# Feed-forward of a decoder layer: token sums in place, down-weight sums made in the up part, sample sums in other banks

## The chip, the cores and the metric

The kernel runs on one core of one Trainium2 chip. The metric is device time in microseconds (us). Before the change it is 1657.48 us, the median of three runs (1655.96 to 1666.1). The core has five engines that run side by side: TensorE (PE), VectorE (DVE), ScalarE (ACT), GpSimd (POOL) and SyncE (SP), which here only issues DMA transfers. Each engine takes its instructions in the order in which they are written; between engines, order is made by semaphores: one instruction adds to a count, another engine waits until the count is reached.

## The reference, cut to what matters

The program is one layer of a decoder: a mixer (retention and latent attention), then a gated feed-forward with a convolution, then a final norm. The change is in the feed-forward alone. It works on 1072 tokens: 16 meta and 1024 prompt tokens, and 32 sample tokens (8 samples of 4), with D = 1024 and F = 2816.

```python
def conv_ffn(h, buf, w_up, conv_w, conv_b, w_down):
    u = h @ w_up                                  # 1024 -> 2 * 2816
    up = jnp.concatenate([buf, u], axis=1)
    c = conv_b
    for j in range(3):                            # causal, one weight per column
        c = c + conv_w[j] * up[:, j:j + T]
    a, g = jnp.split(c, 2, axis=-1)
    y = (jax.nn.silu(g) * a) @ w_down             # 2816 -> 1024
    return y, up[:, up.shape[1] - 2:]
```

Around it stand the norm ahead of it, the residual, h + y, and the last RMSNorm, all in float32.

## The kernel before, in words

**Arithmetic.** A float32 product is made of three matmuls. Each operand is split into a high part (a copy rounded to the matmul type, made by ACT) and a low part (operand minus high part, made by DVE or POOL); hi x hi, hi x lo and lo x hi are added up. On top of that, both big products are cut into 2 x 2 blocks and done by seven block products in place of eight, in the order `PRODUCTS = ("m1", "m5", "m6", "m3", "m7", "m2", "m4")`, called p = 0 to 6. For that, sums and differences of the blocks of both operands are needed.

**Up part.** 22 steps (n = 0 to 21), each for 128 columns of the a half and 128 of the g half of `w_up`. Tokens are in two halves of 532. Steps 0 and 1 are done without the block trick (`plain_part`), steps 2 to 21 with it (`step`). The normed tokens lie in SBUF as `xh` and `xl`; their block sums, four blocks (0 to 3) of four slices of 128x532, are made once, into `th` (high) and `tl` (low): by DVE (`t_slice`, L2489 to L2509: blocks 0, 1 and 3 of slice k), POOL (`t3_slice`, L2191 to L2197: block 2) and ACT (`t_hi`, L2337 and L2340: the high parts), while TensorE works on the plain steps. `tmp`, where sums are worked out, has room for four slices and lies in the same memory (`scr`) as `raw_d`, the down weights for the samples, and beside `chain`. TensorE's p = 1 of step 2 waits for all 16 low parts.

One up step: SP loads the weights into `raw` (`load_up`, L2033, two transfers of 512 KB), once all splits of the step before are done, since there is one `raw`. POOL makes four sums of 128x512 (`sums`, L2149, L2151, L2154, L2155), the middle ones in place in `chain`, so that each waits for the split of the one before; ACT makes seven high parts (`hi_part`, L2271), DVE seven low parts (`lo_part`, L2475), TensorE seven products of 24 matmuls (`passes`, L2699 to L2702). ACT copies PSUM to `u` (`first_out`, L2285, `second_out`, L2299), DVE adds the other products to it (`add_second`, L2517, `add_first`, L2524); p = 5 of the next step waits for `add_second`, as it writes the bank that is read there. Then follow the convolution (`tap2` on ACT, `taps` on DVE), `silu` (ACT), `gate` (DVE), and SP stores the step's rows of the activation into DRAM (`store_act`, L2039, 512 KB). POOL also does small work (`keep`, `params`).

**Samples.** Their down product is not in block form. ACT copies the samples' columns of two steps into `few` (`few_part`, L2330). SP loads two blocks of 128 rows of `w_down` (`load_down`, L2047, 1 MB) into `raw_d`, and TensorE runs 4 narrow matmuls at four column positions into PSUM bank 6 (`strips`, L2776), after every second step. In the down part DVE copies the bank out (`quads`, L2661), TensorE adds the four strips up (`sum_few`, L2800) in banks 4 and 5 (`SUM_BANKS`), and DVE adds `hs`, the residual (L2667); the first matmul of p = 1 waits for that (`few_added`).

**Down part.** 77 steps, `STEPS`: p = 0 to 6 and for each t = 0 to 10. In a step SP loads up to three blocks of 128x512, 256 KB each, into `lanes` (L2110, a ring of four per lane) from the activation in DRAM and from `w_down`; those of p = 0 go to `ka` and `kb` and are kept (L2086, L2087). DVE joins two blocks where the operand is a sum (`join`: activation L2568 to L2577, weights L2583 to L2588); ACT makes the high parts of both operands (`split_d`, L2364 and L2366), DVE the low part of the activation (`lo_a`, L2593), POOL that of the weights (`lo_w`, L2209), each into a ring of four (`NR`); TensorE runs 12 matmuls of 128x512 (`tile_passes`, L2807 to L2809). DVE adds finished products to `y_acc` (`add_piece`, L2601) and norms the rows (`norm_rows`, L2613).

The weight joins of the four products, by lane and kept block:

```python
if p in (1, 2):
    dve.wait_ge(S["lo_w"], i - HF + 1)
    m = dve.tensor_tensor(kb[:, t, :], lane_slot(i, 1), kb[:, t, :], ALU.subtract)
elif p == 4:
    lane_arrived(dve, i, 2)
    m = dve.tensor_tensor(lane_slot(i, 1), lane_slot(i, 1), lane_slot(i, 2), ALU.subtract)
else:
    m = dve.tensor_tensor(lane_slot(i, 1), lane_slot(i, 1), kb[:, t, :], ALU.subtract)
```

Between the parts, SP's order is: last `store_act`, the 22 loads of `ka` and `kb` with the wait for step 20's rows ahead of them, the first lanes, `hs`, `y_acc`, then lanes as they come free.

## Time and profile before

| | |
|---|---|
| runs, median (lowest to highest) | 1657.48 us (1655.96 to 1666.1) |
| the profiled execution: time, span | 1660.88 us, 1659.2 us |
| TensorE busy; weight loads | 1499.5 us (90%); 1275.2 us (77%) |
| VectorE | 835.9 us (50%) |
| ScalarE | 592.4 us (36%) |
| GpSimd | 528.3 us (32%) |
| DMA | 186.77 MB, 113 GB/s in the mean |
| up weights, each of 44 loads | 512 KB, 4.5 us to landing |
| down weights for the samples, each of 11 loads | 1024 KB, 6.0 us |

An engine's busy time is the union of its instructions' spans; register, branch, semaphore and DMA-issuing instructions are not in it. The granted clock (PEclk) is the share of full speed that TensorE had in a stretch. The span runs from the first to the last instruction, and the execution's time is a little longer than it. In the timeline an instruction's line is that of the kernel's file, "out<-in" names the tiles, and the bracket tells how long the engine stood idle before it and what it waited for; SPq is SP's queue, whose entries are DMA issues. The feed-forward begins at about 890 us of the span and fills the rest of it.

### The profile page before, as it was taken

The page shows a single profiled execution, that of the slowest core. Times are in us where ns is not written, and L with a number is a line of the kernel's source. Part 1 is how long each engine was busy: PE and PEld are TensorE (multiplying, and loading weights), DVE is VectorE, ACT ScalarE, POOL GpSimd, SP SyncE. Part 2 cuts the span into 40 slices and gives each one's busy share as a digit, 9 for nine tenths or more (in the row PEclk, how much of TensorE's full clock was granted, in tenths as well). Part 3 has the DMA queues.
Part 4 walks back from the last instruction along what each step waited for, and adds up shares of the span by engine and source line. Part 5 has one row for each costly group of instructions (what it writes and reads, how often), then busy time and mean ns, then how long its engine had stood idle before and what let it go on. Part 6 is the DMA issues. An engine that isn't in the chain of part 4 may idle for free. (4 is left out here: it accounts for less than half of the span.)

```text
span 1659.2 us, 26246 instructions
## 1 busy us (share of the span) xinstructions
PE 1499.5 (90%) x9453; PEld 1275.2 (77%) x9453; DVE 835.9 (50%) x1393; ACT 592.4 (36%) x1267; POOL 528.3 (32%) x620
## 2 busy tenths in 40 slices
PE   5999999695998988886997789999999999999997
PEld 5988888574667876554886779999999999677776
DVE  4422200254416663331146946566666656688877
ACT  5420021032323332321033344444544444533454
POOL 3235620200211005332202444444444433334452
PEclk9999999787998998997998899999999999999999
DMA  6422121535112005544232033333322234854764
GB/s 232 138 95 92 52 98 41 168 102 193 39 32 67 1 1 146 145 128 118 70 111 91 1 102 102 102 101 101 101 88 94 84 101 163 282 168 143 237 213 161
DMA packets 142974, 186.77 MB, mean 113 GB/s; under 512 B 22819, under 2 KB 89236, under 8 KB 142694
## 3 DMA queue, kind: packets, MB, share of 16 engines
q1 hardware_dynamic: 137022, 174.37, 32.8%
q0 software_dynamic: 4800, 9.84, 2.1%
q10 hardware_dynamic: 1056, 1.31, 0.3%
q8 instruction: 56, 0.92, 0.2%
q14 instruction: 40, 0.33, 0.1%
HBM read 149.25 MB, written 36.19 MB: 112 GB/s over the span
## 5 line engine op out<-in xcount | busy, mean ns | idle before, releaser
L2699 PE MATMUL p_ff<-s_xh,s_ff_rhi 128*128 128x266 f32 x608 | 178.8, 294 | 32.9 <-ACT s_ff_u L2285 16.5
L2699 PE MATMUL p_ff<-s_ff_th,s_ff_rhi 128*128 128x266 f32 x640 | 183.8, 287 | 0.0
L2702 PE MATMUL p_ff<-s_ff_th,s_ff_rlo 128*128 128x266 f32 x640 | 183.5, 287 | 0.0
L2701 PE MATMUL p_ff<-s_ff_tl,s_ff_rhi 128*128 128x266 f32 x640 | 183.1, 286 | 0.0
L2702 PE MATMUL p_ff<-s_xh,s_ff_rlo 128*128 128x266 f32 x608 | 176.6, 290 | 0.0
L2701 PE MATMUL p_ff<-s_xl,s_ff_rhi 128*128 128x266 f32 x608 | 176.5, 290 | 0.0
L117 PE MATMUL p_ip<-s_ip_hi,s_xh 128*128 128x512 f32 (+2 forms) x432 | 160.9, 373 | 1.4 <-DVE s_xl L214 1.4
L119 PE MATMUL p_ip<-s_ip_hi,s_xl 128*128 128x512 f32 (+2 forms) x432 | 160.5, 372 | 0.0
L118 PE MATMUL p_ip<-s_ip_lo,s_xh 128*128 128x512 f32 (+2 forms) x432 | 160.3, 371 | 0.0
L2699 PEld LDWEIGHTS p_ff<-s_xh,s_ff_rhi 128*128 128x128 f32 x608 | 117.6, 193 | 43.8 <-issue 22.2
L2807 PE MATMUL p_ff<-s_fd_wh,s_fd_ah 128*128 128x512 f32 x308 | 125.1, 406 | 11.5 <-POOL s_fd_wl L2209 7.1
L2699 PEld LDWEIGHTS p_ff<-s_ff_th,s_ff_rhi 128*128 128x128 f32 x640 | 121.4, 190 | 1.3 <-issue 0.2
L2808 PE MATMUL p_ff<-s_fd_wl,s_fd_ah 128*128 128x512 f32 x308 | 121.9, 396 | 0.0
L2809 PE MATMUL p_ff<-s_fd_wh,s_fd_al 128*128 128x512 f32 x308 | 121.6, 395 | 0.0
L2701 PEld LDWEIGHTS p_ff<-s_ff_tl,s_ff_rhi 128*128 128x128 f32 x640 | 120.9, 189 | 0.0
L2702 PEld LDWEIGHTS p_ff<-s_ff_th,s_ff_rlo 128*128 128x128 f32 x640 | 120.8, 189 | 0.0
L2702 PEld LDWEIGHTS p_ff<-s_xh,s_ff_rlo 128*128 128x128 f32 x608 | 117.5, 193 | 0.0
L2701 PEld LDWEIGHTS p_ff<-s_xl,s_ff_rhi 128*128 128x128 f32 x608 | 117.5, 193 | 0.0
L2475 DVE TENSOR_TENSOR s_ff_rlo<-s_ff_scr,s_ff_rhi 128x512 fp32r<-128x512 f32 x60 | 49.2, 821 | 101.0 <-ACT s_ff_rhi L2271 100.6
L340 POOL TENSOR_TENSOR s_ip_lo<-s_ip_raw,s_ip_hi 128x512 fp32r<-128x512 f32 (+2 forms) x48 | 58.3, 1221 | 110.0 <-ACT s_ip_hi L378 110.0
L117 PEld LDWEIGHTS p_ip<-s_ip_hi,s_xh 128*128 128x128 f32 x432 | 81.8, 189 | 14.3 <-DVE s_xl L214 1.8
L118 PEld LDWEIGHTS p_ip<-s_ip_lo,s_xh 128*128 128x128 f32 x432 | 81.8, 189 | 12.7
(309 smaller groups left out, 3297.0 us busy)
## 6 DMA issues: line engine op xcount, KB each, us to landing
s_ff_raw<-in_w_up SPq DMA_DIRECT2D x44, 512.0 KB, 4.5
s_fd_lanes<-in_w_down SPq DMA_DIRECT2D x77, 256.0 KB, 3.3
s_fd_lanes<-a_rows SPq DMA_DIRECT2D x66, 256.0 KB, 3.1
a_rows<-s_ff_cv SPq DMA_DIRECT2D x22, 512.0 KB, 3.0
s_ff_scr<-in_w_down SPq DMA_DIRECT2D x11, 1024.0 KB, 6.0
s_ip_raw<-in_w_in SPq DMA_DIRECT2D x4, 2048.0 KB, 8.5
s_pages<-in_cache_kv_latent SPq DMA_DIRECT2D x60, 128.0 KB, 2.2
s_pages<-in_cache_kv_latent POOLq DMA_DIRECT2D x52, 128.0 KB, 2.5
```

The source lines that it names most:

```text
L117: pe.matmul(out, hi_w, hi_x, start=first, stop=False)
L118: pe.matmul(out, hi_w, lo_x, start=False, stop=False)
L119: return pe.matmul(out, lo_w, hi_x, start=False, stop=last)
L340: pool.tensor_tensor(w_lo[:, g % 2, k, 0:w], w_raw[:, k, 0:w], w_hi[:, g % 2, k, 0:w].bitcast(F32), ALU.subtract).then_inc(lo_split, 1)
L2475: dve.tensor_tensor(rlo[:, s, :], split_source(n, p), rhi[:, s, :].bitcast(F32), ALU.subtract).then_inc(S["lo"], 1)
L2699: pe.matmul(out, rhi[:, s, ks_], hi_cols(k), start=first and k == 0, stop=False, skip_group_check=True)
L2701: pe.matmul(out, rhi[:, s, ks_], lo_cols(k), start=False, stop=False, skip_group_check=True)
L2702: mm = pe.matmul(out, rlo[:, s, ks_], hi_cols(k), start=False, stop=last and k == 3, skip_group_check=True)
L2807: pe.matmul(out, ah[:, r, ts], wh[:, r, :], start=first, stop=False, skip_group_check=True)
L2808: pe.matmul(out, ah[:, r, ts], wl[:, r, :], start=False, stop=False, skip_group_check=True)
L2809: return pe.matmul(out, al[:, r, ts], wh[:, r, :], start=False, stop=last, skip_group_check=True)
```

## The change

Token sums. Each slice of a block is worked out in its own room: `t1_slice(k)` on DVE makes block 0 in `tmp[:, k]` with three operations in place, `next_slice(1, k)` turns it into block 1 in the same room with two, and `next_slice(3, k)` into block 3. `t3_slice(k)` on POOL does block 2 in a room of its own, `t3_raw`, over a part of `th` that is written last. All 16 low parts are now made by POOL (`t_lo`), the high parts by ACT one by one (`t_hi(block, k)`) in the order `T_ORDER`. TensorE waits at p = 1, 2, 4 and 6 of step 2 for 4, 8, 12 and 16 low parts.

Down weights. `raw_d` now takes rows t and t + 11 (of blocks of 128) together, which are the two block rows of `w_down`, and only from step 12 on, one such load in each step. POOL makes four differences of them in place between its sums (`join_first` two of them, `join_third`, `join_fourth`), once the strips have read the weights, and SP stores the result, 1 MB, to a new DRAM tensor `t_rows`. The down part loads these as the weight operand in p = 1, 2, 4 and 6; its 44 weight joins on DVE and the third lane of p = 4 are gone.

Samples. `few` holds the sample columns of all first eleven steps, written by POOL (`few_part`), and `few_pair` puts those of steps t and t + 11 beside each other in `few_now`. The strips run between p = 2 and p = 3 of TensorE's steps 12 to 21, the last ones after down step 3 as before. The sample sums use banks 7 and 6, one down step earlier; `hs` has a semaphore of its own, and TensorE waits for `few_added` only at the third tile of p = 1.

The diff, cut to its core:

```diff
 SP
-                    load_down(q)                                  (end of pair)
+                def load_down(t):
+                    if isinstance(t, int) and t == 0:
+                        sp.wait_ge(S["t_hi"], 16)
+                        sp.wait_ge(S["t_lo"], 16)
+                    wait_past(sp, S["wt_stored"], t * 16)
+                    sp.dma_start(raw_d, w_pairs[bass.ds(t * P, P)]).then_inc(S["wd"], 16)
+                def store_joined(t):
+                    sp.wait_ge(S["wt_joined"], t * 4 + 4)
+                    sp.dma_start(t_rows[bass.ds(t * P, P), :], scr[:, 0:2 * D]).then_inc(S["wt_stored"], 16)
+                def full_pair(q):
+                    load_up(q * 2 + 1)
+                    load_down(q * 2 - HF - 1)
+                    store_act(q * 2 - 1)
+                    store_joined(q * 2 - HF - 1)
+                    load_up(q * 2 + 2)
+                    load_down(q * 2 - HF)
+                    store_act(q * 2)
+                    store_joined(q * 2 - HF)
...
                 load_up(NF - 1)
+                load_down(HF - 3)
                 store_act(NF - 3)
-                load_down(PAIRS - 1)
+                store_joined(HF - 3)
+                load_down(HF - 2)
                 store_act(NF - 2)
+                store_joined(HF - 2)
+                load_down(HF - 1)
                 (the loads of ka and kb)
...
-                        return {1: w_block(t, False, 1), 2: w_block(t, True, 1), 3: w_block(t, True, 1),
-                                4: w_block(t, True, 1), 5: w_block(t, True, 0), 6: w_block(t, True, 0)}[p]
+                        return {1: t_block(t, 0), 2: t_block(t, 3), 3: w_block(t, True, 1), 4: t_block(t, 1),
+                                5: w_block(t, True, 0), 6: t_block(t, 2)}[p]
...
+                sp.wait_ge(S["wt_stored"], 16 * (HF - 1))
+                sp.dma_start(hs[:], h_rows[0:NS, :]).then_inc(S["hs_in"], 16)
                 for i in range(HF, HF + NL):
                     load_lanes(i)
+                store_joined(HF - 1)
+                sp.wait_ge(S["wt_stored"], 16 * HF)
 POOL, sums(n, t)
                     pool.tensor_tensor(chain, A21, A22, ALU.add).then_inc(S["sums"], 1)
+                    if t is not None:
+                        join_first(t)
                     pool.wait_ge(S["lo"], done + 2)
                     pool.tensor_tensor(chain, chain, A11, ALU.subtract).then_inc(S["sums"], 1)
+                    if t is not None:
+                        join_third(t)
                     pool.wait_ge(S["sums"], base + 2)
                     pool.wait_ge(S["lo"], done + 3)
                     pool.tensor_tensor(chain, A12, chain, ALU.subtract).then_inc(S["sums"], 1)
                     pool.tensor_tensor(A21, A11, A21, ALU.subtract).then_inc(S["sums"], 1)
+                    if t is not None:
+                        join_fourth(t)
+                def join_first(t):
+                    pool.wait_ge(S["few_done"], t + 1)
+                    pool.tensor_tensor(b11, b12, b11, ALU.subtract).then_inc(S["wt_joined"], 1)
+                    pool.tensor_tensor(b12, b22, b12, ALU.subtract).then_inc(S["wt_joined"], 1)
+                def step(n, m, early):
+                    if early:
+                        few_part(n - 1)
+                    else:
+                        few_pair(n - 1)
+                    sums(n + 1, None if early else n - HF - 1)
...
 POOL, order at the start
+                t3_slice(0); t_lo(0, 0); t3_slice(1); t_lo(0, 1); keep(0, 0); t3_slice(2); params(1, 1, 0)
+                t_lo(0, 2); t_lo(0, 3); t3_slice(3); keep(0, 1); params(1, 1, 1); t_lo(1, 0..3); t_lo(2, 0..3)
+                few_part(0); sums(2); keep(1, 0); keep(1, 1); params(2, ..); t_lo(3, 0..3); step(2, 0, True)
 POOL, order at the end
+                step(NF - 2, 0, False); few_pair(NF - 2); join_first, third, fourth(HF - 2); lo_w(0..3)
+                keep(NF - 1, ..); lo_w(4); few_pair(NF - 1); lo_w(5..7); join_first, third, fourth(HF - 1); lo_w(8..)
 ACT, order at the start (few_part is gone from ACT)
+                hi_part(0, 0..3); t_hi(0, 0); first_out(0, 0, 0); t_hi(0, 1); hi_part(1, 0..2); second_out(0, 0, 0)
+                tap2(0, 0, 0); first_out(0, 0, 1); t_hi(0, 2); t_hi(0, 3); second_out(0, 0, 1); tap2(0, 0, 1)
+                hi_part(1, 3); silu(0); first_out(1, 1, 0); t_hi(1, 0..3); second_out(1, 1, 0); t_hi(2, 0..3)
+                hi_part(2, 0..1); tap2(1, 1, 0); first_out(1, 1, 1); hi_part(2, 2); second_out(1, 1, 1); tap2(1, 1, 1)
+                hi_part(2, 3); first_out(2, 0, 0); t_hi(3, 0..3); hi_part(2, 4..6); step(2, 0)
 DVE, order at the start
+                lo_part(0, 0..3); t1_slice(0..1); lo_part(1, 0..2); taps(0, 0, 0); t1_slice(2..3); taps(0, 0, 1)
+                lo_part(1, 3); next_slice(1, 0..3); gate(0); lo_part(2, 0..1); next_slice(3, 0); taps(1, 1, 0)
+                lo_part(2, 2); next_slice(3, 1); lo_part(2, 3); taps(1, 1, 1); next_slice(3, 2..3); lo_part(2, 4..6)
 DVE, join(i): the four branches for "w" are gone
-                    if i == HF + 3:
-                        dve.wait_ge(S["h_in"], 16 * (1 + KD))
+                    if i == HF + 2:
+                        dve.wait_ge(S["hs_in"], 16)
+                        if p == 1 and t == 4:
+                            dve.wait_ge(S["h_in"], 16 * KD)
 PE
                     for p in range(7):
+                        if p == 3 and not early:
+                            strips(n - HF - 1)
...
-                                pe.wait_ge(S["t_lo_dve"], 12)
-                                pe.wait_ge(S["t_lo_pool"], 4)
+                                pe.wait_ge(S["t_lo"], 4)           (p = 1; 8, 12, 16 at p = 2, 4, 6)
-                step(2, 0)
-                strips(0)                                          (and after every second step)
...
                             elif p == 1:
-                                pe.wait_ge(S["few_added"], 2)
+                                pe.wait_ge(S["ua1b"], NF - 2)
+                                pe.wait_ge(S["st_out"], NBATCH)
+                                if m >= 2:
+                                    pe.wait_ge(S["few_added"], 2)
```

In the orders at the start and at the end, `0..3` stands for a loop and `;` for a new line.

## Rows read from the trace of the kernel before

**Rows 1.** Table of stretches: start:end, us, busy by engine (instructions), PEclk, DMA share, GB/s

```profile
986.66:1186.15 199.49, 196.16 (x1552) 189.91 (x1553) 122.64 (x153) 96.06 (x171) 82.56 (x109) 0.99 0.32 98
1186.15:1381.82 195.67, 193.66 (x1546) 188.23 (x1545) 124.69 (x153) 96.01 (x171) 83.57 (x109) 1.00 0.30 94
1381.82:1410.07 28.25, 28.23 (x225) 27.06 (x225) 16.65 (x22) 13.53 (x24) 10.46 (x14) 1.00 0.51 180
...
1447.43:1584.44 137.01, 129.35 (x529) 99.07 (x529) 117.54 (x138) 55.23 (x100) 56.17 (x43) 0.98 0.58 183
```

**Rows 2.** Table of waits on TensorE, 890 to 1660: us in total, times, longest

```profile
PE p_ff L2699 <- ACT s_ff_u L2285: 16.5, 2, 12.0
PE p_ff L2699 <- DVE s_ff_u L2517: 8.4, 9, 3.1
...
PE p_ff L2807 <- POOL s_fd_wl L2209: 7.1, 19, 3.0
...
PE p_ff L2807 <- DVE s_fd_hs L2667: 2.7, 1, 2.7
```

**Rows 3.** Timeline of two up steps: start, us, engine, line, operation [idle before <-releaser]

```profile
1213.67 1.06 PE L2776 MATMUL p_ff<-s_ff_scr,s_ff_few 128*32 128x512 f32 x8
...
1229.57 0.28 PE L2699 MATMUL p_ff<-s_xh,s_ff_rhi 128*128 128x266 f32 x1
...
1235.57 0.28 PE L2699 MATMUL p_ff<-s_xh,s_ff_rhi 128*128 128x266 f32 x1
...
1238.80 1.00 SPq L2033 DMA_DIRECT2D s_ff_raw<-in_w_up  x2
...
1244.48 0.28 PE L2699 MATMUL p_ff<-s_xh,s_ff_rhi 128*128 128x266 f32 x1
1244.50 1.29 POOL L2149 TENSOR_TENSOR s_ff_scr<-s_ff_raw 128x512 f32<-128x512 f32 x1 [2.78 <-DMA s_ff_raw<-in_w_up]
...
1247.26 1.28 POOL L2151 TENSOR_TENSOR s_ff_scr<-s_ff_scr,s_ff_raw 128x512 f32<-128x512 f32 x1 [1.47 <-DVE s_ff_rlo L2475]
...
1249.85 0.71 DVE L2517 TENSOR_TENSOR s_ff_u<-p_ff,s_ff_u 128x532 f32<-128x532 f32 x1
...
1250.71 0.36 PE L2699 MATMUL p_ff<-s_xh,s_ff_rhi 128*128 128x266 f32 x1 [0.15 <-DVE s_ff_u L2517]
```

**Rows 4.** Timeline while the token sums are built, VectorE and GpSimd

```profile
902.87 0.70 DVE L2490 TENSOR_TENSOR s_ff_scr<-s_xl 128x532 f32<-128x532 f32 x1
...
908.77 1.87 POOL L2191 TENSOR_TENSOR s_ff_scr<-s_xh 128x532 f32<-128x532 f32 x1 [6.39 <-ACT s_ff_th L2340]
...
909.87 4.81 DVE L2475 TENSOR_TENSOR s_ff_rlo<-s_ff_raw,s_ff_rhi 128x512 fp32r<-128x512 f32 x3 [0.43 <-ACT s_ff_rhi L2271]
```

**Rows 5.** Timeline at the start of the up steps, SP and TensorE

```profile
974.58 0.99 SPq L2033 DMA_DIRECT2D s_ff_raw<-in_w_up  x2
...
986.66 0.36 PE L2699 MATMUL p_ff<-s_xh,s_ff_rhi 128*128 128x266 f32 x1 [3.07 <-DVE s_ff_u L2517]
```

**Rows 6.** Timeline of SP; then DMA issues: KB each, us to landing

```profile
901.30 52.70 SPq L2033 DMA_DIRECT2D s_ff_raw<-in_w_up  x4
...
955.30 0.37 SPq L2047 DMA_DIRECT2D s_ff_scr<-in_w_down  x1
...
s_ff_scr<-in_w_down SPq DMA_DIRECT2D x1, 1024.0 KB, 7.2
...
a_rows<-s_ff_cv SPq DMA_DIRECT2D x19, 512.0 KB, 2.9
```

**Rows 7.** Table of stretches, the 3 us behind the wait of rows 5

```profile
987.00:990.00 3.00, 3.00 (x20) 3.00 (x19) 1.99 (x3) 1.26 (x2) 1.55 (x2) 0.70 0.00 0
```

**Rows 8.** Timeline of the down part, product p = 3, VectorE and GpSimd

```profile
1536.81 1.20 DVE L2574 TENSOR_TENSOR s_fd_lanes<-s_fd_lanes,s_fd_ks_early 128x512 f32<-128x512 f32 x1
...
1539.34 1.30 POOL L2209 TENSOR_TENSOR s_fd_wl<-s_fd_lanes,s_fd_wh 128x512 fp32r<-128x512 f32 x1 [1.88 <-ACT s_fd_wh L2366]
...
1539.98 1.20 DVE L2574 TENSOR_TENSOR s_fd_lanes<-s_fd_lanes,s_fd_ks_late 128x512 f32<-128x512 f32 x1
```

More of the change, by code:

```diff
@@ L1919, in conv_ffn @@
         K = ("a", "g")
+        T_ORDER = [(b, k) for b in range(4) for k in range(4)]
         PRODUCTS = ("m1", "m5", "m6", "m3", "m7", "m2", "m4")
@@ L2220, in _ @@
                 pool.wait_ge(S["pad"], 1)
-                for k in range(4):
-                    t3_slice(k)
+                t3_slice(0)
+                t_lo(0, 0, tmp[:, 0, :])
+                t3_slice(1)
+                t_lo(0, 1, tmp[:, 1, :])
                 keep(0, 0)
+                t3_slice(2)
                 params(1, 1, 0)
+                t_lo(0, 2, tmp[:, 2, :])
+                t_lo(0, 3, tmp[:, 3, :])
+                t3_slice(3)
                 keep(0, 1)
                 params(1, 1, 1)
+                for k in range(4):
+                    t_lo(1, k, tmp[:, k, :])
+                for k in range(4):
+                    t_lo(2, k, t3_raw[:, k, :])
+                few_part(0)
                 sums(2)
@@ L2231, in _ @@
                 params(2, 0, 1)
-                step(2, 0)
-                step(3, 1)
-                with pool.Fori(2, PAIRS - 1) as it:
-                    step(it * 2, 0)
-                    step(it * 2 + 1, 1)
-                step(NF - 2, 0)
+                for k in range(4):
+                    t_lo(3, k, tmp[:, k, :])
+                step(2, 0, True)
+                step(3, 1, True)
+                with pool.Fori(2, HF // 2) as it:
+                    step(it * 2, 0, True)
+                    step(it * 2 + 1, 1, True)
+                step(HF - 1, 0, True)
+                step(HF, 1, True)
+                with pool.Fori(HF // 2 + 1, PAIRS - 1) as it:
+                    step(it * 2, 0, False)
+                    step(it * 2 + 1, 1, False)
+                step(NF - 2, 0, False)
+                few_pair(NF - 2)
+                join_first(HF - 2)
+                join_third(HF - 2)
+                join_fourth(HF - 2)
                 for i in range(4):
@@ L2241, in _ @@
                 keep(NF - 1, 1)
-                for i in range(4, len(STEPS)):
+                lo_w(4)
+                few_pair(NF - 1)
+                for i in range(5, 8):
+                    lo_w(i)
+                join_first(HF - 1)
+                join_third(HF - 1)
+                join_fourth(HF - 1)
+                for i in range(8, len(STEPS)):
                     lo_w(i)
@@ L2591, in lo_a @@
+                    m.then_inc(S["joined"], 1)
                 def lo_a(i):
@@ L2757, in step @@
                         else:
+                            if isinstance(n, int) and n == 2:
+                                pe.wait_ge(S["t_lo"], 16)
                             pe.wait_ge(S["ug2b"], n - 1)
```

310 lines of the change are left out of this document (159 added, 151 removed).

## Prediction

> **What bounds the kernel now.** First the page's busy shares and its 40 slices: TensorE is busy 90% of the span and nearly all of the feed-forward, so I read who makes it wait, stage by stage. In the table of stretches I cut at a recurring mark, the first matmul of product m2 (p = 5) of a step: the nine steps up to 1186.15 take 199.49 us, the next nine 195.67 us, and the granted clock there is 0.99 to 1.00 [rows 1]. The table of waits shows what is left to gain on TensorE from 890 us on: 16.5 us in two gaps while the token sums are built, 8.4 us in nine waits at p = 5, 7.1 us for down weights, 2.7 us for the sample sums [rows 2].
>
> The timeline of one step shows why the up part runs at 21.7 us a step. From p = 5 at 1229.57 TensorE needs 6.00 us to the next step (1235.57) and 8.91 us more for p = 0 to 2 (1244.48). Beside it runs a loop that is as long: p = 5, then 9.23 us later (1238.80) SP issues the next up weights, 5.70 us later they are there and POOL starts the first sum (1244.50), then sum, ACT split, DVE split, next sum, and DVE's add of L2517 (1249.85), which p = 5 needs: 1250.71, a loop of 21.14 us [rows 3]. So in the up part anything that is put into this loop costs time, though POOL is busy only 43% of it.
>
> VectorE and GpSimd do not overlap on everything. Three splits of DVE took 4.81 us from 909.87 while POOL's subtraction at 908.77 took 1.87 us; apart they take 0.70 us and 1.28 us each [rows 3, 4]. They take turns: a DVE operation with both inputs in SBUF waits for POOL's, and the other way round.
>
> **Part 1, token sums.** DVE goes from 40 operations to 28 (12 in t1_slice, 16 in next_slice), POOL from 16 to 28 (12 in t3_slice, 16 in t_lo). In shared turns that is 12 x 1.28 more and 12 x 0.70 less, +7 us, of which the last four t_lo (5 us) lie behind the point that counts. The new order takes first_out(0, 0, 1) out from behind the third slice, so the 12.0 us gap goes, and load_up(2) is issued some 18 us earlier. But TensorE's place at 986.66 was not set by that gap: it waits 3.07 us there for the add that hangs on load_up(3), issued at 974.58, 12.08 us before [rows 5]. That issue needs all of step 2's splits, and in the new order hi_part(2, 4..6) stands behind four t_hi(3, k), those behind next_slice(3, 3), that behind taps(1, 1, 1); the POOL sums stand behind eight t_lo (8 x 1.28 plus DVE's turns). Walking the four queues with these durations I get load_up(3) at 976 to 977. I take **+2 us**; the ends are -5 (DVE's turns all fall into gaps) and +6 (they all collide).
>
> **Part 2, steps 3 to 11.** The strips leave these steps (1.06 us in every second, [rows 3]) and few_part moves from ACT to POOL, in the wait before the first sum. The loop of 21.14 stays and becomes the bound, 0.15 us of latency on top: eight steps at 21.3 instead of 21.99, the first about 0.3 shorter: **-6 us** (ends -10, TensorE alone; 0, every second step as long as now).
>
> **Part 3, steps 12 to 20: the down weights in the up part.** Each step gets a 1 MB load, a strip, four POOL operations of 128x512 and a 1 MB store. The load is issued on SP right behind load_up, and the strip that needs it has moved between p = 2 and p = 3.
> - The load. There is one row of a down load queued behind up weights: load_up's pair issued at 953.0 (the merged row ends at 954.00, a pair is 1.00), a 0.5 MB store after it, the down load at 955.30, landed 7.2 us later, 962.5, so 9.5 us after load_up's issue [rows 3, 6]. Without the store (0.5 MB, about 1.3 us of transfer) it is 8.2; I take 8.0, with ends 7.4 and 8.4. From p = 5: 9.3 + 8.0 = 17.3. TensorE comes to the strip at 6.00 + 8.91 = 14.9. **So TensorE waits about 2.4 us in every step**, and behind it p = 3 to 6.
> - The joins. join_first waits for few_done, and POOL's second sum is queued behind it. Strip done at 17.3 + 1.1 + 0.1 = 18.5; two joins 2.5, second sum 1.3 (22.3); join_third 1.25 is issued before DVE's split gets its turn, split 0.55, add 0.65, 0.15 to TensorE: p = 5 at 24.9. TensorE alone would be there at 18.4 + 0.15 + 2 x 2.96 = 24.5. After that join_fourth holds up lo_part 4 and add_first by 0.75, which shifts the next load_up: 24.9 to 25.65, and I take 25.6 us a step.
> - Nothing hides this: DVE, ACT and SP all hang on p = 5. The store of 1 MB goes out 4 us after p = 5 and is down by about 9, before the next load (10.4), so it costs nothing here.
>
> Nine steps: 9 x 25.6 = 230.4 against 195.67, **+34.7 us**. Ends: if the load is never late, the joins alone give 23.2 + 0.75 = 23.95, +20; if DVE and POOL did not take turns either, 22.4, +6; load at 8.4 and a clock drop in each step, 26.6, +44.
>
> The clock: the wait of 3.07 us was followed by a granted clock of 0.70, that is a stretch at 1.2 instead of 2.4 GHz [rows 5, 7]; the eight other waits of that kind (8.4 - 3.1, so 0.7 us each) lie in stretches of 0.99 to 1.00 [rows 1, 2]. 2.4 us lies between, nearer to the one that dropped; I price it at nothing in the forecast because no row has it, and as a rival below. The Trainium skill, "TensorE: Matmul & The Clock Gate", section "HAM oscillation", says that a loop which waits for a DMA in every tile can start every tile on the lower clock. By it each of the nine steps would pay, and the sum would be 17 us higher; the rows here show only the two ends.
>
> **Part 4, into the down part.** Now the first down loads go out after store_act(20). In the new order SP first waits for join_fourth(9), stores 1 MB, waits for it, and loads 1 MB. From p = 5 of step 20: strip 9 at 16.1, four joins 5.1 (21.3), store landed 4.2 to 5 later (0.5 MB takes 2.9, [rows 6]), so 25.7, then ka and kb behind 1 MB: 31, splits of ACT and POOL 2.7: 33.7. TensorE is free at 28.1 (28.25 now, [rows 1]). A wait of 5.6 us and a slow clock after it, 1.9: **+7.5 us** (+4 to +11). few_pair, join_first(10) and its two followers on POOL fall where lo_w runs ahead by the ring of four: nothing.
>
> **Part 5, the down part.** The 44 w joins leave DVE. What they are worth is read where none of them runs: in p = 3 there is only the a join, and it still starts every 3.17 us (1536.81, 1539.98), blocked by POOL's lo_w at 1539.34 each time, as ACT's next split waits for the join [rows 8]. Steps 11 to 53, 137.01 us [rows 1], are 3.19 each: the same pace. So the removal leaves this lock-step and gains about 1 us. The sample sums, in other banks and one step earlier, take away the wait of 2.7 and the slow clock behind it, 2; the last step no longer waits for a w join, 3.0 to about 1, and the clock behind it, 1.6 [rows 2]. **-9 us** (-4; -16 if the w joins were the cause).
>
> **Sum.** +2 - 6 + 34.7 + 7.5 - 9 = +29 us. The profiled execution took 1660.88 us (span 1659.2), which gives 1690; the median of the three runs is 3.4 lower, so 1657.5 + 29 = **1687 us**.
>
> **Rivals.**
> - All hidden. If the load lands in time (it does if it starts beside load_up without delaying it) and POOL's 57% of idle time takes the joins, part 3 is 22.0 a step, +2.5, part 4 nothing, and part 5 the full -16: 1657.5 + 2 - 6 + 2.5 - 16 = **1640**, faster. For it speaks POOL's idle time; against it that the idle time lies inside the loop. 0.10.
> - Joins but no late load: part 3 +20, part 4 +6: 1657.5 + 2 - 6 + 20 + 6 - 9 = **1671**. It decides if the two loads together land by 14.9 after p = 5, 5.6 after load_up's issue; load_up alone is there at 5.7. 0.20.
> - A clock drop in every step: 1687 + 9 x 1.9 = **1704**. It decides if TensorE's wait reaches what dropped it at 986.66. 0.20.
> - The edit does not do what it says: the token sums could gain the 16.5 us of the two gaps if load_up(3) came as early as load_up(2): 1687 - 16 = 1671. Against it the queues of part 1. 0.05.
>
> The forecast has 0.45. 1% is 16.6 us, about what a measurement of this kernel can tell from no change. Below 1641 lies the first rival, 0.10; within 1% the second, the fourth and a little of the forecast's own lower end, 0.27; above 1674 the rest, 0.63. The range 1655 to 1708 leaves out the fast rival and the upper end of the clock rival.
>
> **What would show it.** Right: TensorE idle 2 to 3 us before L2776 of steps 12 to 20, released by the DMA of the down weights; p = 5 to p = 5 at 25 to 26 us there and 21.3 before; the join of p = 3 still every 3.2 us; a gap of about 6 us before the first down matmul. Wrong: steps of 22 us after step 12, or p1 to p4 of the down part at 2.75 us a step. Then part 3 or part 5 has the wrong sign.

## The result and the profile after

The change makes the kernel slower: 1714.57 us, the median of four runs (1711.75 to 1721.29), against 1660.97 of the four runs of before (the three above and one more); the ratio is 1.033 (95% interval 1.029 to 1.037). The forecast was 1687, range 1655 to 1708: the sign is right, the size is not, and the time lies above the range.

The profiled execution after has a span of 1711.0 us, 51.8 more than before. Cut at the same marks as before (p = 5 of a step; the first down matmul; the last line holds p = 1 to 4 of the down part, 44 steps), the table of stretches answers to [rows 1]:

```profile
983.25:1179.70 196.45, 193.03 (x1513) 190.38 (x1513) 120.98 (x153) 93.72 (x162) 84.74 (x118) 0.99 0.24 73
1179.70:1426.15 246.45, 213.16 (x1584) 201.04 (x1585) 128.85 (x153) 94.14 (x163) 135.31 (x163) 0.93 0.38 130
1426.15:1467.43 41.28, 30.18 (x226) 29.00 (x225) 17.96 (x23) 14.11 (x24) 18.75 (x22) 0.83 0.60 219
...
1506.44:1643.24 136.80, 129.12 (x529) 96.37 (x528) 101.23 (x107) 55.79 (x102) 56.41 (x43) 1.00 0.54 166
```

Steps 3 to 11 take 196.45 us (199.49 before), steps 12 to 20 take 246.45 (195.67) at a granted clock of 0.93 where it was 1.00, and from p = 5 of step 20 to the first down matmul it is 41.28 (28.25). The down part from there to the end is 243.6 (249.1): its first 11 steps are 4.1 us shorter, p = 1 to 4 are 2.7 us longer (134.12 before), and the end is 4.2 shorter. The first matmul of the up part came at 894.33 against 899.49, so 5.2 us of the difference lie ahead of the change; in the other executions shown below that matmul lies anywhere between 893.8 and 903.3, whatever the kernel. From it to p = 5 of step 2 it is 88.9 us against 87.2. So the account of the profiled executions is -5.2 (not the change's) + 1.7 - 3.0 + 50.8 + 13.0 - 5.6 = 51.7.

The table of waits on TensorE, from 880 us on, names the two large ones (answers to [rows 2]):

```profile
PE p_ff L2874 <- DMA s_ff_scr<-in_w_down: 33.0, 9, 4.6
PE p_ff L2792 <- DVE s_ff_u L2611: 18.3, 11, 11.1
```

**One of the nine slow steps**, in the timeline (start, us, engine, line, operation; to be held against [rows 3]):

```profile
1317.62 0.29 PE L2792 MATMUL p_ff<-s_xh,s_ff_rhi 128*128 128x266 f32 x1
...
1326.80 1.03 SPq L2037 DMA_DIRECT2D s_ff_raw<-in_w_up  x2
1328.13 1.06 SPq L2052 DMA_DIRECT2D s_ff_scr<-in_w_down  x1
...
1331.86 0.37 SPq L2043 DMA_DIRECT2D a_rows<-s_ff_cv  x1
...
1336.46 1.22 PE L2874 MATMUL p_ff<-s_ff_scr,s_ff_few_now 128*32 128x512 f32 x8 [3.81 <-DMA s_ff_scr<-in_w_down]
1337.61 0.59 PE L2792 MATMUL p_ff<-s_xh,s_ff_rhi 128*128 128x266 f32 x1
1337.78 1.27 POOL L2263 TENSOR_TENSOR s_ff_scr<-s_ff_scr 128x512 f32<-128x512 f32 x1 [3.81 <-PE p_ff L2874]
...
1340.24 1.29 POOL L2184 TENSOR_TENSOR s_ff_scr<-s_ff_scr,s_ff_raw 128x512 f32<-128x512 f32 x1
...
1342.03 0.29 PE L2792 MATMUL p_ff<-s_ff_th,s_ff_rhi 128*128 128x266 f32 x1
...
1343.24 0.70 DVE L2611 TENSOR_TENSOR s_ff_u<-p_ff,s_ff_u 128x532 f32<-128x532 f32 x1
...
1345.00 0.29 PE L2792 MATMUL p_ff<-s_xh,s_ff_rhi 128*128 128x266 f32 x1
```

Read it from p = 5 to p = 5: 9.18 us to the issue of the up weights, 9.66 from there until the down weights are there and the strips start, 1.15 for the strips, 4.42 for p = 3 (1337.61 to 1342.03), 2.97 for p = 4: 27.38. TensorE stood idle 3.81 us ahead of the strips. The add that p = 5 needs (1343.24) is done a microsecond before p = 5 starts, so in this step TensorE is the bound behind the strips, and p = 3 is slow because of its clock (what that costs stands at experiment 3):

```profile
1336.46:1339.00 2.54, 2.54 (x14) 1.55 (x15) 0.00 (x0) 0.00 (x0) 1.23 (x1) 0.65 0.06 23
...
1342.03:1345.00 2.97, 2.97 (x26) 2.97 (x25) 1.72 (x2) 0.44 (x2) 2.34 (x3) 1.00 0.00 0
```

**Between the parts** stands one wait of 11.1 us, and it is not where it was expected:

```profile
1445.35 0.71 DVE L2611 TENSOR_TENSOR s_ff_u<-p_ff,s_ff_u 128x532 f32<-128x532 f32 x1 [5.26 <-PE p_ff L2795]
1447.57 0.33 SPq L2056 DMA_DIRECT2D t_rows<-s_ff_scr  x1
1451.43 0.39 SPq L2052 DMA_DIRECT2D s_ff_scr<-in_w_down  x1
1451.92 0.41 SPq L2114 DMA_DIRECT2D s_fd_ka<-a_rows  x1
...
1458.52 0.63 ACT L2466 ACTIVATE s_fd_ah<-s_fd_ka 128x512 fp32r<-128x512 f32 x1 [16.68 <-DMA s_fd_kb<-in_w_down]
...
1459.18 0.69 DVE L2677 TENSOR_TENSOR s_fd_al<-s_fd_ka,s_fd_ah 128x512 fp32r<-128x512 f32 x1 [13.12 <-ACT s_fd_ah L2466]
...
1461.49 0.70 DVE L2611 TENSOR_TENSOR s_ff_u<-p_ff,s_ff_u 128x532 f32<-128x532 f32 x1
1462.34 0.56 PE L2792 MATMUL p_ff<-s_ff_th,s_ff_rhi 128*128 128x266 f32 x1 [11.11 <-DVE s_ff_u L2611]
```

VectorE adds the first product of step 21 at 1445.35. The next add, L2611 at 1461.49, stands behind two low parts for the down part (L2677), which wait for ScalarE's high parts, which wait for the first loads of ka and kb, and SP issues these at 1451.92 behind a store and a load of 1 MB. p = 6 of step 21 needs that add.

### The profile page after: what moved, and what is told of

It is laid out like the page before. It is cut to its first block and busy times, and to the rows that moved or that the text cites. A ratio compares the mean times of both kernels' runs of the same rounds, so it can differ in the third digit from the quotient of the medians.

```text
span 1711.0 us, 26234 instructions
## 1 busy us (share of the span) xinstructions
PE 1516.0 (89%) x9453; PEld 1288.0 (75%) x9453; DVE 800.2 (47%) x1337; ACT 585.3 (34%) x1245; POOL 615.7 (36%) x709
## 5 line engine op out<-in xcount | busy, mean ns | idle before, releaser
L2792 PE MATMUL p_ff<-s_xh,s_ff_rhi 128*128 128x266 f32 x608 | 186.3, 306 | 24.8 <-DVE s_ff_rlo L2581 8.1
L2792 PE MATMUL p_ff<-s_ff_th,s_ff_rhi 128*128 128x266 f32 x640 | 185.9, 290 | 15.3 <-DVE s_ff_u L2611 11.1
L2794 PE MATMUL p_ff<-s_xl,s_ff_rhi 128*128 128x266 f32 x608 | 183.8, 302 | 0.0
L2795 PE MATMUL p_ff<-s_xh,s_ff_rlo 128*128 128x266 f32 x608 | 183.0, 301 | 0.0
L2792 PEld LDWEIGHTS p_ff<-s_xh,s_ff_rhi 128*128 128x128 f32 x608 | 124.9, 205 | 37.8 <-issue 29.0
L2792 PEld LDWEIGHTS p_ff<-s_ff_th,s_ff_rhi 128*128 128x128 f32 x640 | 122.9, 192 | 17.4 <-issue 16.5
L2287 POOL TENSOR_TENSOR s_fd_wl<-s_fd_lanes,s_fd_wh 128x512 fp32r<-128x512 f32 x66 | 88.6, 1344 | 113.1 <-ACT s_fd_wh L2468 113.1
L2581 DVE TENSOR_TENSOR s_ff_rlo<-s_ff_scr,s_ff_rhi 128x512 fp32r<-128x512 f32 x60 | 53.8, 896 | 160.9 <-ACT s_ff_rhi L2378 160.7
L2794 PEld LDWEIGHTS p_ff<-s_xl,s_ff_rhi 128*128 128x128 f32 x608 | 125.2, 206 | 0.0
L2795 PEld LDWEIGHTS p_ff<-s_xh,s_ff_rlo 128*128 128x128 f32 x608 | 124.6, 205 | 0.0
```

What stands on the lines that cost most here:

```text
L2287: pool.tensor_tensor(wl[:, i % NR, :], w_operand(i), wh[:, i % NR, :].bitcast(F32), ALU.subtract).then_inc(S["lo_w"], 1)
L2581: dve.tensor_tensor(rlo[:, s, :], split_source(n, p), rhi[:, s, :].bitcast(F32), ALU.subtract).then_inc(S["lo"], 1)
L2792: pe.matmul(out, rhi[:, s, ks_], hi_cols(k), start=first and k == 0, stop=False, skip_group_check=True)
L2794: pe.matmul(out, rhi[:, s, ks_], lo_cols(k), start=False, stop=False, skip_group_check=True)
L2795: mm = pe.matmul(out, rlo[:, s, ks_], hi_cols(k), start=False, stop=last and k == 3, skip_group_check=True)
```

## Experiments

Nine up steps are given from p = 5 of step 11 to p = 5 of step 20: 195.67 us before, 246.45 after. The ratio of a run is to the kernel before, timed beside it.

**1. The down load ahead of the up load.**

```diff
-                    load_up(q * 2 + 1)
                     load_down(q * 2 - HF - 1)
+                    load_up(q * 2 + 1)
                     store_act(q * 2 - 1)
```

(the same for the second step of the pair and at the end)

> The changed kernel with one order swapped on SP: in steps 12 to 20 the load of the down weights is issued ahead of that of the up weights instead of behind it. Theory L (the late load is the price): the load goes out some 7 us after p = 5 and is down before TensorE reaches the strips at 14.9, so the wait of 3.2 to 4.6 us before L2874 is gone and with it the slow clock behind it; p = 5 to p = 5 becomes 22 to 23.3 us instead of 27.4, and the time 1672 to 1680 against 1714.6. Theory J (the joins on GpSimd are the price): the wait moves to p = 5, where the add waits for sums that stand behind the joins, and the step stays at 26 to 27 us, the time above 1700. Theory D (the extra 2 MB a step are the price, wherever they stand): the up weights land 2.5 us later, the step is 25 to 26 us, the time about 1700.

Measured: 1692.86 us (ratio to before 1.019, interval 1.016 to 1.023), nine steps 222.98, 24.8 us each. The waits on TensorE in these steps:

```profile
PE p_ff L2792 <- DVE s_ff_u L2611: 16.3, 10, 3.6
PE p_ff L2874 <- POOL s_ff_few_now L2253: 2.1, 6, 0.7
```

The wait for the load is gone. But the step does not come down to 22 or 23: the wait has moved to p = 5, as theory J said, half as large, and 24.8 us lies below the 26 to 27 of that theory. GpSimd's part of the timeline shows why:

```profile
1247.97 1.28 POOL L2180 TENSOR_TENSOR s_ff_scr<-s_ff_raw 128x512 f32<-128x512 f32 x1 [1.36 <-DMA s_ff_raw<-in_w_up]
1249.21 1.29 POOL L2263 TENSOR_TENSOR s_ff_scr<-s_ff_scr 128x512 f32<-128x512 f32 x1
1250.47 1.73 POOL L2264 TENSOR_TENSOR s_ff_scr<-s_ff_scr 128x512 f32<-128x512 f32 x1
1252.17 1.28 POOL L2184 TENSOR_TENSOR s_ff_scr<-s_ff_scr,s_ff_raw 128x512 f32<-128x512 f32 x1
1253.42 1.27 POOL L2268 TENSOR_TENSOR s_ff_scr<-s_ff_scr 128x512 f32<-128x512 f32 x1
```

The second sum (L2184) starts 4.20 us after the first, with two joins between, and a third join (L2268) stands ahead of the next. A part of the wait is theory D's. The down load waits for the store of the joined weights of the step before, so in steps 13 to 20 it goes out only 1.3 to 3.0 us ahead of the up weights, and these land 5.8 to 8.2 us after their issue, 6.6 in the mean, against 5.6 to 5.9 in the changed kernel. The step with the 8.2 has the longest wait at p = 5, 3.6 us; its first sum starts 8.5 us behind the issue:

```profile
1289.47 0.40 SPq L2052 DMA_DIRECT2D s_ff_scr<-in_w_down  x1
1290.78 1.04 SPq L2037 DMA_DIRECT2D s_ff_raw<-in_w_up  x2
...
1299.25 1.29 POOL L2180 TENSOR_TENSOR s_ff_scr<-s_ff_raw 128x512 f32<-128x512 f32 x1 [2.95 <-DMA s_ff_raw<-in_w_up]
```

**2. Without the joins.** The four `tensor_tensor` and their counts are left out, the store waits for the strips.

> The changed kernel without the four differences per step on GpSimd: the down weights are stored to DRAM as they were loaded, so the operands of p = 1, 2, 4 and 6 of the down part are not the right ones; loads, strips, stores and all else stay. Theory L: the load is as late as before, TensorE still waits 3 to 4.5 us before the strips and p = 3 still runs at the lower clock; the steps are 26 to 27.4 us, the time within 10 us of 1714.6. Theory J: without the joins the steps are 22 to 23 us and the time is about 1670. Theory D: 27 us a step.

Measured, in a single run: 1705.72 us, nine steps 240.17, 26.7 each; TensorE still waits for the down load in all nine, 30.7 us in total. So with the load late, the joins are nearly hidden.

**3. Filler in the wait.**

```diff
+                    for r in range(8):
+                        pe.matmul(banks[:, 7, 0:PIECE], xh[:, r, 0:P], xh[:, r, 0:PIECE], start=True, stop=True, ...)
                     pe.wait_ge(S["wd"], t * 16 + 16)
```

> The changed kernel with 8 matmuls of 128x266 on resident data into an unused bank ahead of TensorE's wait for the down weights in steps 12 to 21: some 3.0 us of work that nothing reads, inside a wait of 3.2 to 4.6 us. It prices the clock by itself. If the slow p = 3 behind the wait (4.4 us in place of 3.0) is what idleness does to the clock, p = 3 takes 3.0 us again and the granted clock of the steps is 0.99; the next thing that is late is then the add in front of p = 5 (as in step 14, where the clock did not fall and the step took 25.8), so the steps are 25.8 to 26.2 instead of 27.4 and the time is 1701 to 1706. If the clock falls for another reason, the step stays at 27.4 and the time at 1714.

Measured: 1713.14 us (1.032, interval 1.029 to 1.036), nine steps 243.26. The filler was shorter than I had meant: eight such matmuls took 1.14 us, not 3.0, and 21.7 us of waiting were left. It did keep the clock up in some steps, and two neighbours show what that is worth. The wait, and the clock of p = 3 behind it:

```profile
1226.68 1.94 PE L2878 MATMUL p_ff<-s_ff_scr,s_ff_few_now 128*32 128x512 f32 x8 [3.38 <-DMA s_ff_scr<-in_w_down]
1228.55:1233.40 4.85, 4.85 (x29) 4.85 (x26) 0.23 (x1) 0.63 (x1) 4.67 (x4) 0.59 0.00 0
...
1254.23 1.06 PE L2878 MATMUL p_ff<-s_ff_scr,s_ff_few_now 128*32 128x512 f32 x8 [1.85 <-DMA s_ff_scr<-in_w_down]
1255.22:1258.26 3.04, 3.04 (x28) 3.04 (x25) 0.00 (x0) 0.00 (x0) 2.85 (x3) 1.00 0.02 5
```

Behind 1.85 us of waiting p = 3 took 3.04 us at a clock of 1.00, behind 3.38 us it took 4.85 at 0.59. Yet the first four steps came in turns, 25.5 us with the good clock, 29.3 with the bad one, then 25.4 and 29.3: their mean is that of the changed kernel. With the good clock the joins, the adds and the splits are as late as TensorE was, so the next loads go out hardly earlier. From the start of the strips to the issue of the next up weights it is 17.4 to 17.5 us where the clock stayed up (four steps, here and in the changed kernel together), 17.5 to 17.7 where p = 3 alone was slow, and 18.4 to 18.8 where the strips were slow as well (1.9 us in place of 1.0). In the changed kernel it is 17.84 in the mean, against 17.46 in the four steps with the good clock, so the clock cost an estimated 0.4 us a step there: it was lost, but it was not what set the pace. Without the joins (experiment 2) it costs more: there the same stretch is 16.1 us in the two steps where the clock stayed up, and 17.5 to 17.8 in the others:

```profile
1229.55 1.06 PE L2862 MATMUL p_ff<-s_ff_scr,s_ff_few_now 128*32 128x512 f32 x8 [3.59 <-DMA s_ff_scr<-in_w_down]
...
1245.62 1.03 SPq L2037 DMA_DIRECT2D s_ff_raw<-in_w_up  x2
...
1308.31 1.06 PE L2862 MATMUL p_ff<-s_ff_scr,s_ff_few_now 128*32 128x512 f32 x8 [3.37 <-DMA s_ff_scr<-in_w_down]
...
1326.03 1.03 SPq L2037 DMA_DIRECT2D s_ff_raw<-in_w_up  x2
```

In the first of these two steps p = 3 took 3.04 us, in the second 4.58.

**4. Joins of the down part one step ahead.**

```diff
                 for i in range(5, len(STEPS)):
-                    join(i)
+                    if i + 1 < len(STEPS):
+                        join(i + 1)
                     lo_a(i)
```

> The changed kernel with one order swapped on VectorE in the down part: the join of step i + 1 is issued ahead of the low part of step i. Theory K (lock-step): p = 1 to 4 run at 3.15 to 3.3 us a step because ScalarE's high part waits for a join that waits for GpSimd's low part, and that for the high part of the step before; with the join one step ahead TensorE is the bound at 2.72 to 2.8, 44 steps become 15 to 20 us shorter and the time is 1695 to 1700. Theory S (VectorE's and GpSimd's operations shut each other out, and 1.2 + 0.7 + 1.3 = 3.2 us of them in a step is the bound): the steps stay at 3.1 to 3.2 and the time at 1710 to 1715.

Measured: 1700.85 us (1.025, interval 1.022 to 1.028), 13.7 less than the changed kernel. p = 1 to 4 run at 2.72 us a step, TensorE's own pace:

```profile
1510.61:1630.29 119.68, 119.68 (x530) 99.10 (x528) 98.63 (x107) 55.92 (x103) 64.62 (x44) 1.00 0.63 196
```

That is 119.68 us for 44 steps against 136.80, and theory K is shown: the same operations in another order, and none of them is in TensorE's way.

**5. Down load first, and no joins** (edits 1 and 2 together).

> Both edits of the first two runs in one: the down weights loaded ahead of the up weights, and the four differences per step left out (the operands of p = 1, 2, 4 and 6 of the down part are then not the right ones). Each alone left the steps at 24.9 and 26.6 us, against 27.4. Theory L+J (the late load and the joins lie one behind the other, and each covers the other in part): with both gone TensorE is the bound again, 8.91 + 6.0 + 1.0 for the strips + 5.94 and a short wait at p = 5, that is 22.0 to 22.3 us, and the time is 1664 to 1670. Theory D (the 2 MB a step cost something by themselves): 23 to 24 us a step, 1674 to 1684.

Measured, in a single run: 1664.27 us; nine steps 198.58, 22.06 each, clock 1.00. Both causes together are the whole loss of these steps but for 0.3 us a step (the strips, 1.06 us, now stand in every step and not in every second). The four corners: 22.06 with neither, 24.8 with the joins alone (the later up weights of experiment 1 among them), 26.7 with the late load alone, 27.4 with both. The two run side by side, so they do not add up, and the late load hides most of the joins.

**6. ka and kb first between the parts.**

```diff
                 store_act(NF - 2)
-                store_joined(HF - 2)
-                load_down(HF - 1)
 ... (loads of ka and kb, t = 0 to 10)
+                    if t == 3:
+                        store_joined(HF - 2)
+                    if t == 7:
+                        load_down(HF - 1)
```

> The changed kernel with another order on SP between the two parts: the loads of ka and kb for t = 0 to 3 go out ahead of the store of the joined weights of step 9, the down load of step 10 behind those of t = 7. Theory Q: the 11.1 us before p = 6 of step 21 are VectorE's add standing behind lo_a(0) and lo_a(1), which wait for loads that SP issues 11 us late; with the loads early the wait is gone, the first down matmul comes 28 to 31 us after p = 5 of step 20 in place of 41.3, and the time is 1701 to 1705 against 1714.6. If the 11.1 us have another cause (the joins on GpSimd, the store's traffic), the first down matmul stays at 38 us or more and the time above 1711.

Measured, in a single run: 1706.56 us. p = 6 of step 21 waits 0.34 us in place of 11.1, and the first down matmul comes 28.9 us after p = 5 of step 20 (1456.34 - 1427.45) in place of 41.3:

```profile
1453.30 0.36 PE L2794 MATMUL p_ff<-s_ff_th,s_ff_rhi 128*128 128x266 f32 x1 [0.34 <-DVE s_ff_u L2613]
...
1456.34 0.40 PE L2907 MATMUL p_ff<-s_fd_wh,s_fd_ah 128*128 128x512 f32 x1
...
1460.19 0.50 PE L2907 MATMUL p_ff<-s_fd_wh,s_fd_ah 128*128 128x512 f32 x1 [2.31 <-ACT s_ff_u L2394]
```

Theory Q holds, for the wait and for the first down matmul. Inside the first down step 2.3 us of waiting for a copy out of PSUM stay, which in the kernel before was 0.9.

**7. The kernel before with joins ahead** (edit 4 on it, weight joins and all).

> The kernel before, with all joins (of the activation and of the weights) of step i + 1 on VectorE issued ahead of the low part of step i in the down part. It asks what taking the weight joins off VectorE is worth once the lock-step is gone. If the lock-step is all, p = 1 to 4 go from 3.05 us to 2.72 as in the changed kernel with joins ahead, 44 steps gain 14 us and the time is 1642 to 1647. If VectorE with three operations a step beside GpSimd's is too much (0.7 + 0.7 + 0.7 and 1.3 in turns, 3.4 us), the products with a weight join (p = 1, 2, 4) stay at 3.0 or above and the time is 1652 to 1658; then the weight joins are worth what p = 3 gains more than these.

Measured: 1652.30 us (0.995, interval 0.993 to 0.997). Its 44 steps of p = 1 to 4 take 122.10 us, 2.78 each, with 44 weight joins on VectorE. But the wait for the sample sums ahead of p = 1 grew from 2.7 to 6.7 us, so a third of these 12.0 us was lost there.

**8. Strips and joins later.** In steps 12 to 20 the strips go between p = 4 and p = 5, and all four joins behind GpSimd's fourth sum.

> The changed kernel with two places moved in steps 12 to 20: the strips stand between p = 4 and p = 5 of TensorE instead of between p = 2 and p = 3, 5.9 us later, and GpSimd makes all four differences behind its fourth sum instead of between the sums. By theory L+J the load, down 18.7 us after p = 5, is then ahead of the strips (20.9), and the joins run in GpSimd's idle time from 1.3 to 6.5 us behind p = 5, so the steps are 22.0 to 22.8 us; the wait into the down part may grow by 5, as the last joins come later. Time 1672 to 1682. If joins slow VectorE's splits and taps wherever they run, the steps are 24 us or more and the time above 1684.

Measured: 1685.69 us (1.016, interval 1.012 to 1.019), nine steps 214.02, 23.8 each, clock 1.00. The wait for the load is gone, but the joins cost 1.7 us a step here too (against the 22.06 of experiment 5), in GpSimd's idle time:

```profile
1255.39 1.59 DVE L2623 SCALAR_TENSOR_TENSOR s_ff_cv<-s_ff_u,s_ff_now,s_ff_cv 128x1072 f32<-128x1072 f32 x1 [0.70 <-ACT s_ff_cv L2424]
1255.92 2.22 POOL L2270 TENSOR_TENSOR s_ff_scr<-s_ff_scr 128x512 f32<-128x512 f32 x1
1257.01 2.26 DVE L2627 SCALAR_TENSOR_TENSOR s_ff_cv<-s_ff_u,s_ff_now,s_ff_cv 128x1072 f32<-128x1072 f32 x1
```

The fourth join took 2.22 us (1.28 alone) and the convolution's operations beside it 1.59 and 2.26 (1.33 alone): VectorE and GpSimd take turns, as in [rows 3, 4], and from step 13 on the up weights go out 10.9 to 11.2 us behind p = 5 in place of 9.2. They also land later behind their issue, 6.2 to 6.7 us, as the store of the joined weights goes out just ahead of them; how the 1.7 us divide between the two is not shown.

**9. Token sums alone** on the kernel before.

> The kernel before with the token sums of the change alone (and the first down load for the samples behind the up load of step 3 in place of ahead of it, as it now waits for all 16 low parts). In the changed kernel p = 5 of step 2 came 3.4 us earlier than before and steps 3 to 11 took 3.0 us less, where +2 and -6 had been expected. If the token sums bring the 3.4 us by themselves, p = 5 of step 2 lies at 983 to 984 against 986.7 and the time is 3 to 4 us lower, 1654 to 1656; the nine steps behind stay at 199 to 200 us, as the strips still stand in every second one. If the 3.4 us come from the few_part and the load that left these steps, p = 5 of step 2 stays at 986 to 988 and the time at 1658 to 1660.

Measured: 1662.55 us (1.001, interval 0.999 to 1.003). From the first up matmul to p = 5 of step 2 it is 87.2 us, as before (987.06 - 899.82). The 3.4 us were not the token sums' doing; they lay ahead of the feed-forward.

**10. Sample sums and joins ahead** on the kernel before, without token sums and without work on down weights.

> The kernel before with the sample sums of the change (banks 7 and 6, one down step earlier, a semaphore of their own for hs, the wait at the third tile) and the joins one step ahead. With the joins ahead alone, the wait for the sample sums ahead of p = 1 grew from 2.7 to 6.7 us and took back half of the gain. If that wait goes, with the slower clock behind it, the time is 1643 to 1647; if the sample sums still hold up p = 1, 1649 to 1653.

Measured: 1647.94 us (0.993, interval 0.991 to 0.996): below both kernels, and 0.7% below the kernel before.

**11. All three**: with the token sums as well.

> The kernel before with the token sums, the sample sums and the joins one step ahead, and without any of the work on down weights in the up part. The parts add up if none of them hides another: 1643 to 1647 from the two, 3 to 4 less for the token sums, that is 1639 to 1644, faster than both kernels. If the token sums are worth nothing, 1643 to 1647.

Measured: 1650.31 us (0.993, interval 0.991 to 0.996). The token sums add nothing: it is 2.4 us more than without them, and the intervals overlap.

**12. The changed kernel with repairs 8, 6 and 4.**

> The changed kernel with the three repairs that leave its plan as it is: the strips between p = 4 and p = 5 with the joins behind GpSimd's fourth sum (steps of 24.0 us in place of 27.4, 1685.7 by itself), the loads of ka and kb ahead of the last stores (6 to 8 us in one look), and the joins of the down part one step ahead (14 us). If the three losses are separate, they add up to 1714.6 - 29 - 7 - 14 = 1662 to 1667: still not below the kernel before, because the joins hold VectorE up in nine steps by 2 us each and the weight joins that they replace cost VectorE nothing (1658.6 and 1652.3 were measured with them in place). If they hide one another, 1670 or more; if a part of the loss was counted twice, 1655 or less.

Measured: 1659.03 us (0.999, interval 0.997 to 1.001), level with before and a little better than the sum: with ka and kb early and the last joins late, the way into the down part is 32.7 us.

## Why the prediction was wrong

**What bounds the kernel now** was read rightly: TensorE, with the loop over the up load as long beside it, and what is put into that loop costs time.

**Part 1** had +2 and measured +1.7, counted from the first up matmul, and that the two agree is in part luck. In the eleven profiled executions that hold the token sums, this stretch is 87.2 to 89.2 us, in the three without them 87.2 to 87.9, so they cost 0 to 2 us; in experiment 9 they cost nothing. The path was read rightly: counted in the same way, the up load of step 2 went out 17.9 us earlier and that of step 3 1.5 us later, and p = 5 still hung on the add behind it. But the gap of 12.0 us did not simply go: TensorE's gaps in this stretch are now 6.1, 2.6, 3.4, 1.5 and 3.5 us, 17.1 in all, where they were 19.6.

**Part 2** had -6 and measured -3.0: the loop runs at 21.6 us a step, not 21.3. p = 5 waits 0.2 to 0.6 us for the add in eight of these nine steps, so it is the bound named. The row taken for every step had the up weights issued 9.23 us behind p = 5; they went out 9.4 to 9.6 us behind it.

**Part 3 is the step that failed**, in the size of one term, the time from the issue of the up weights to the landing of the down weights. The part gave +50.8 for +34.7, outside its ends (+6 to +44). The mechanism was there in each of nine steps, TensorE waiting for the down load ahead of L2874, but the wait was 3.7 us (33.0 / 9), not 2.4. The row read for it said 9.5 us [rows 3, 6]; I took 1.3 off for the store that stood between, a saving that no run shows, and took 8.0. Measured are 9.0 to 9.8, 9.5 in the mean. The store had not gone: SP issues it at 1331.86, while the load is under way, and the queue moved 2.56 MB in the 9.62 us from 1326.80 to the landing, as it had moved 2.62 MB in the 9.51 us of the row. The row as it stood was the price. The forecast's own chain with 9.5 in place of 8.0 gives 27.1 us a step, where 27.4 were measured.

The second miss, a small one, is the clock, which the forecast priced at nothing and a rival at 1.9 us a step: in eight of the nine steps p = 3 took 4.4 to 4.8 us in place of 3.0, at a clock of 0.65 where it is shown above. By the Trainium skill, "TensorE: Matmul & The Clock Gate", section "HAM oscillation", a loop that waits for a DMA in each tile can start each tile on the lower clock; eight of nine steps here did so. It cost an estimated 0.4 us a step (experiment 3), because the add and the splits were about as late.

The third number, the chain of the joins behind the strips, was right: 7.6 us from the strips to p = 5 in the forecast (17.3 to 24.9), and 7.5 in step 14, where the add held p = 5. With the load early (experiments 1 and 5) the joins cost 2.7 us a step, and the end named "the joins alone" had 23.95 us where 24.8 were measured, the later up weights of experiment 1 among them.

The rivals were each half right. "Joins but no late load" is experiment 1. "A clock drop in every step" saw the drop, in eight of nine steps, but its price of 1.9 us a step was too high: 1.4 to 1.7 without the joins (16.1 against 17.5 to 17.8 in experiment 2) and 0.4 with them.

**Part 4** had +7.5 (+4 to +11) and measured +13.0. The late loads of ka and kb were foreseen (first loads at 25.7 behind p = 5 of step 20; measured 1451.92 - 1426.15 = 25.8), and what they hold up first was not: VectorE's order has lo_a(0) and lo_a(1) ahead of an add of step 21, so the wait came already inside step 21, at p = 6, and its 3 us of matmuls and the slow clock (together 5.1 us) came on top. I named who waits for the loads, and not what is queued behind the waiting instruction.

**Part 5** had -9 and measured -5.6. The sample sums brought 4.1 in the first 11 steps and 2.0 in p = 1, where the slow clock behind the old wait is gone, 6.1 where 4.7 were forecast; the end brought 4.2 where 3.6 were. But p = 2 to 4, with 22 of the 44 weight joins taken off VectorE there, became 4.7 us slower, where about 1 us less had been forecast. The pace of 3.19 that I read for the kernel before was too high, since the stretch held the wait for the sample sums and 44 steps (10 to 53), not 43; p = 1 to 4 without that wait are at 3.05.

Step by step, the lock-step of [rows 8] has the same pace in both kernels, 3.1 to 3.2 us, but the kernel before is in it in 17 of the 33 steps of p = 2 to 4 and the changed one in 31. A weight join does not always keep it away: five of the 17 are in p = 2 and five in p = 4. In the first steps of p = 4 of the kernel before it does, and the timeline runs like this:

```profile
1558.44 1.78 DVE L2586 TENSOR_TENSOR s_fd_lanes<-s_fd_lanes 128x512 f32<-128x512 f32 x1
...
1560.74 0.68 DVE L2577 TENSOR_TENSOR s_fd_lanes<-s_fd_ka,s_fd_lanes 128x512 f32<-128x512 f32 x1
...
1560.96 1.61 POOL L2209 TENSOR_TENSOR s_fd_wl<-s_fd_lanes,s_fd_wh 128x512 fp32r<-128x512 f32 x1 [1.30 <-ACT s_fd_wh L2366]
1561.34 1.79 DVE L2586 TENSOR_TENSOR s_fd_lanes<-s_fd_lanes 128x512 f32<-128x512 f32 x1
```

Here it is the weight join (L2586) that meets GpSimd's low part and takes 1.79 us, while the activation's join (L2577) runs in 0.68, and a step takes 2.9. After the change only the join that ScalarE waits for is left in this product, and it meets the low part each time, at 3.18 us a step:

```profile
1616.72 1.31 POOL L2287 TENSOR_TENSOR s_fd_wl<-s_fd_lanes,s_fd_wh 128x512 fp32r<-128x512 f32 x1 [1.87 <-ACT s_fd_wh L2468]
1616.77 1.81 DVE L2672 TENSOR_TENSOR s_fd_lanes<-s_fd_ka,s_fd_lanes 128x512 f32<-128x512 f32 x1
...
1618.67 0.63 ACT L2466 ACTIVATE s_fd_ah<-s_fd_lanes 128x512 fp32r<-128x512 f32 x1 [2.03 <-DVE s_fd_lanes L2672]
```

So the lock-step was right, and that it holds in every step before as after was wrong: in these steps the work taken away had shielded the join on the path. That the order of the join makes the lock-step is shown by experiments 4 and 7; that the missing weight joins are why the changed kernel hardly leaves it is read from these steps alone, as no run puts them back by themselves.

**Of the signs** that were named, two held: the idle time ahead of the strips is released by the down load (3.2 to 4.6 us for 2 to 3), and the join of p = 3 still starts every 3.2 us (3.18). The steps were longer than the sign said, 27.4 for 25 to 26, and 21.6 for 21.3 ahead of them; the gap between the parts was 11.1 us for 6, and it stood ahead of p = 6 of step 21 and not of the first down matmul. The range failed on the same term: part 3's upper end had the clock dropping in each step, but the load at 8.4 us, and so 26.6 us a step. The five upper ends together (+6, 0, +44, +11, -4) are +57 us, that is 1714.5; the range stopped at 1708 and was narrower than its own parts.

Two things stay open. No run moves the store in these steps, so that its bytes are the 1.5 us is read from the amount that the queue moved, and not shown; and no run shows what the missing weight joins cost by themselves. That p = 2 of the down part is at 3.3 us a step after the change comes from one step of 4.54 us, in which VectorE's last operation on the sample rows (L2697, 2.16 us) stands ahead of a join; the others take 3.13 to 3.22.

## What to carry to other kernels

Price a queued transfer by the row that shows it queued, and take off nothing for a neighbour that will still be in flight. When work is moved into a loop that is already as long as the main engine's step, try first the order of issue in it: here one swap on SP gave back 22 us, and one on VectorE 14. Before an operation is taken off an engine, look whether it is the one that waits there; if the operation on the path takes its place in the queue, issue that one a step ahead instead, which brought 6.3 us on the kernel before (experiment 7), with all its weight joins in place.

## What was not expected of the hardware

Waits of nearly the same length were followed by different clocks: 3.25 us ahead of the strips of step 14 by a p = 3 of 3.07 us, 3.22 us ahead of those of step 19 by one of 4.58. Nor did the longer wait always drop it: in experiment 1 a wait of 2.06 us ahead of p = 5 was followed by a clock of 0.64, one of 2.36 us by 1.00. And a 1 MB load took 8.3 us to landing behind 1 MB of up weights, but 4.9 to 5.3 ahead of them (experiment 1, steps 13 to 20), where what it cost them went with its lead: with 3.0 us of lead they landed 5.8 to 5.9 us after their issue, with 2.1 to 2.4 us 6.2 to 6.9, and with 1.3 us 8.2.
